# Differential attention of the last two layers moved beside the projection of the banded queries

## The reference

```
h    = rmsnorm(x, g_attn);  proj = h @ w_in          # 2304 columns
qa, ka, va, qb, kb, vb = split(proj)                 # 512, 128, 128, 512, 512, 512
qa, ka, qb, kb = rope(rmsnorm per head of 64)
ya = banded attention(qa, ka, va, sink)              # 8 heads, 2 key heads, blocks |i-j| <= 1 of 128 tokens
s1, s2 = softmax(qb1 kb1'), softmax(qb2 kb2')        # 4 heads, each with two score maps over all 512 tokens
yb = (s1 - lam * s2) @ vb;  yb = rmsnorm(yb, subln) * (1 - lambda_init)
x  = x + [ya, yb] @ w_out
x  = x + (silu(conv(h2 @ w_gate)) * (h2 @ w_up)) @ w_down
```

## Time and profile before

| what | us |
| --- | --- |
| median of 3 runs (2639.18 to 2640.3) | 2639.46 |
| the profiled execution | 2639.93 |
| its span | 2638.1 |
| PE busy | 2494.4 (95%) |
| DVE busy | 1500.0 (57%) |
| ACT busy | 905.5 (34%) |
| POOL busy | 228.1 (9%) |

### The profile page before, as it was taken

One profiled execution on the slowest core, in us unless ns is written; L12 is line 12 of the kernel. 1 busy time (PEld: TensorE's weight loads), 2 busy tenths in 40 slices (PEclk: granted clock), 3 DMA queues, 4 the chain that ended last, 5 costly groups with the idle time before them and its releaser, 6 DMA issues.

```text
span 2638.1 us, 31556 instructions
## 1 busy us (share of the span) xinstructions
PE 2494.4 (95%) x12844; PEld 2050.2 (78%) x12844; DVE 1500.0 (57%) x2120; ACT 905.5 (34%) x1340; POOL 228.1 (9%) x157
## 2 busy tenths in 40 slices
PE   7997999999998799999999779999999888999999
PEld 6766788888876688888887567888888666888887
DVE  5866543434587654343458774646465866554554
ACT  4361322222436133222253553322234354322222
POOL 2002200000210220000042002000002200100000
PEclk9988999999998999999999899999999988999999
DMA  4200122232320012222222001222232200222222
GB/s 172 81 17 1 49 96 100 92 109 87 112 77 33 1 48 96 96 96 96 96 96 96 33 1 64 96 96 96 96 111 97 96 1 1 96 96 96 96 96 96
DMA packets 30241, 205.37 MB, mean 78 GB/s; under 512 B 3344, under 2 KB 3728, under 8 KB 6032
## 3 DMA queue, kind: packets, MB, share of 16 engines
q1 hardware_dynamic: 30096, 203.35, 22.0%
HBM read 201.24 MB, written 2.10 MB: 77 GB/s over the span
## 4 chain that ended last, share of the span: by engine, by line
PE 86%; DVE 9%; DVEq 2%; ACT 2%; issue 1%; POOL 0%; ACTq 0%; DMA 0%; SPq 0%
PE bank L1344 24%; PE bank L1345 24%; PE bank L1346 24%; PE bank L1470 2%; PE bank L1494 2%; PE bank L1451 2%; PE bank L1426 1%; DVE a_conv L917 1%; DVE w_lo L661 1%; PE bank L1632 1%; PE bank L1671 1%; DVE b_p L1216 1%; PE bank L1481 1%; PE bank L1768 1%; DVE neg_max L1204 1%
## 5 line engine op out<-in xcount | busy, mean ns | idle before, releaser
L661 DVE TENSOR_TENSOR w_lo<-w_raw,w_hi 128x2048 fp32r<-128x2048 f32 (+1 forms) x190 | 433.8, 2284 | 418.1 <-ACT w_hi L312 417.9
L1344 PE MATMUL bank<-h_ffn_hi,w_hi 128*128 128x512 f32 x1408 | 548.6, 390 | 0.0
L1346 PE MATMUL bank<-h_ffn_hi,w_lo 128*128 128x512 f32 x1408 | 547.8, 389 | 0.0
L1345 PE MATMUL bank<-h_ffn_lo,w_hi 128*128 128x512 f32 x1408 | 547.8, 389 | 0.0
L312 ACT ACTIVATE w_hi<-w_raw 128x2048 fp32r<-128x2048 f32 (+1 forms) x190 | 360.0, 1895 | 539.9 <-PE bank L1346 491.6
L1346 PEld LDWEIGHTS bank<-h_ffn_hi,w_lo 128*128 128x128 f32 x1408 | 264.3, 188 | 55.1
L1345 PEld LDWEIGHTS bank<-h_ffn_lo,w_hi 128*128 128x128 f32 x1408 | 264.3, 188 | 54.7
L1344 PEld LDWEIGHTS bank<-h_ffn_hi,w_hi 128*128 128x128 f32 x1408 | 264.3, 188 | 54.6
L1344 PE MATMUL bank<-act_hi,w_hi 128*128 128x512 f32 x704 | 273.9, 389 | 0.0
L1345 PE MATMUL bank<-act_lo,w_hi 128*128 128x512 f32 x704 | 273.9, 389 | 0.0
L1346 PE MATMUL bank<-act_hi,w_lo 128*128 128x512 f32 x704 | 273.9, 389 | 0.0
(11 more groups left out here) (303 smaller groups left out, 3561.3 us busy)
## 6 DMA issues: line engine op xcount, KB each, us to landing
w_raw<-weights SPq DMA_DIRECT2D x188, 1024.0 KB, 4.7
residual<-x_in SPq DMA_DIRECT2D x8, 256.0 KB, 6.3
x_out<-residual SPq DMA_DIRECT2D x8, 256.0 KB, 2.1
cst<-consts SPq DMA_DIRECT2D x1, 960.0 KB, 10.6
par_b<-params_b SPq DMA_DIRECT2D x1, 627.0 KB, 11.6
par_a<-params_a SPq DMA_DIRECT2D x1, 244.0 KB, 2.6
w_raw<-weights SPq DMA_DIRECT2D x2, 64.0 KB, 2.0
```

Of the source, the lines that this page charges most:

```text
L661: nc.vector.tensor_tensor(w_lo[s][:, cols], w_raw[s][:, cols], w_hi[s][:, cols].bitcast(F32), ALU.subtract).then_inc(w_ready, 1)
L1344: mm(out, ahi, bhi, start=start, stop=False)
L1345: mm(out, ahi, blo, start=False, stop=False)
L1346: return mm(out, alo, bhi, start=False, stop=stop)
```

## The change

Only the third and fourth layer change, with some set-up at the start.

- The order of the weight groups becomes qb (g0, g0+1), kb (g0+2, 3), vb (g0+4, 5), ka and va (g0+6), qa (g0+7, 8).
- DVE does `tables` behind `split_lo(g0+2)`, and two ropes of qb ahead of `split_lo(g0+3)`.
- The turns of qb stand behind the four half groups of vb, those of kb beside the group of ka and va.
- The differential loop comes first. Behind the PE work of each of its steps 0 to 3 stand two blocks of the qa projection (12 matmuls of 512 columns each). ACT empties them in steps 2 and 3 (`evict_queries`), POOL squares them (`query_squares`, formerly ACT), DVE sums the squares in steps 4, 6, 8, 10 (`stat_a`) and ropes them in steps 5, 7, 9, 11 (`rope_a`); the six turns of ka and qa stand behind steps 11 to 13, in banks 2 and 3.
- Scores use banks 5 and 6 alone up to step 4, then these and 0 and 1 in turn; transposes use bank 7 alone, the output bank 4 alone.
- The banded loop follows, and `norm_diff(3)` and `mix_ready` fall into its step 3.
- lam of both layers is computed once at the start, its four vectors by a transfer of their own; the masks are made from the comparison masks, so `cst` is 128 KB smaller.

The core of the diff (set-up, overlays of tiles and renamed tiles left out):

```diff
 # DVE, layers three and four
+                norm_stats(2 * lay)
+                split_lo(g0 + 2)
+                tables(par, B["b_table_b"], [(B_QB, HD ** -0.5), (B_KB, 1.0)], C_ROPE + 2 * TB * HD, 1)
+                tables(par, B["b_table_a"], [(B_QA, HD ** -0.5), (B_KA, 1.0)], C_ROPE + 2 * TB * HD, 1)
                 if l == 0:
                     norm_bc(2 * lay)
                     for k in range(KT):
                         nc.vector.scalar_tensor_tensor(residual[:, k, :], ...)
+                rope_b(0, 0)
+                rope_b(0, 1)
                 split_lo(g0 + 3)
+                rope_b(0, 2)
+                rope_b(0, 3)
                 split_lo(g0 + 4)
+                rope_b(1, 0)
+                rope_b(1, 1)
                 split_lo(g0 + 5)
+                key_lo(0)
+                rope_b(1, 2)
                 split_lo(g0 + 6)
+                key_lo(1)
+                rope_b(1, 3)
+                key_lo(2)
+                key_lo(3)
                 split_lo(g0 + 7)
+                for m in range(4, 8):
+                    key_lo(m)
+                for i in range(19):
+                    if i < 16:
+                        diff_max(i)
+                    if 1 <= i <= 16:
+                        diff_coef(i - 1)
+                    if i >= 6 and i % 4 == 2:
+                        t = (i - 6) // 4
+                        take_diff(t)
+                        if t >= 1:
+                            norm_diff(t - 1)
+                    if i == 0:
+                        split_lo(g0 + 8)
+                    if i == 3:
+                        split_lo(g0 + 9)
+                    if 4 <= i < 11 and i % 2 == 0:
+                        stat_a((i - 4) // 2)
+                    if 5 <= i < 9 + 3 and i % 2 == 1:
+                        rope_a((i - 5) // 2)
+                    if i == 12:
+                        split_lo(g0 + 10)
+                    if 11 <= i < 14:
+                        for n in (2 * (i - 11), 2 * (i - 11) + 1):
+                            tile_lo(8 + n, tb, ..., banks=(2, 3))
 # ACT, in the differential loop
+                    if i == 1:
+                        split_hi(g0 + 9)
+                    if i in (2, 3):
+                        evict_queries(i - 2)
+                    if i == 3:
+                        split_hi(g0 + 10)
+                    if 11 <= i < 14:
+                        for n in (2 * (i - 11), 2 * (i - 11) + 1):
+                            tile_hi(8 + n, tb, ..., banks=(2, 3))
 # POOL
+                def query_squares(t):
+                    pool.wait_ge(qa_raw, 4 * l + t + 1)
...
+                    nc.gpsimd.tensor_tensor(B["b_qsq"][:, 0:512], q, q, ALU.mult)
+                    nc.gpsimd.tensor_tensor(B["b_qsq"][:, 512:640], k, k, ALU.mult).then_inc(qsq_done, 1)
 # PE
+                pe.wait_ge(rope_ready, 8 + 12 * l + 4)
+                for second in range(2):
+                    enter(g0 + 4 + second)
+                    for half in range(2):
+                        pair_half(g0 + 4, second, half)
+                        m = 2 * second + half
+                        turn(m, base, lambda t: B["b_qb"][:, t, m * P:(m + 1) * P])
+                enter(g0 + 6)
+                token_half(g0 + 6, 0)
+                pe.wait_ge(rope_ready, 8 + 12 * l + 8)
+                for m in range(4):
+                    turn(4 + m, base, lambda t: B["b_kb"][:, t, m * P:(m + 1) * P])
+                    if m == 1:
+                        token_half(g0 + 6, 1)
+                for i in range(19):
...                     # scores of i, transposes of i-2, value product of i-3
+                    if i < 4:
+                        if i % 2 == 0:
+                            enter(g0 + 7 + i // 2)
+                        for n in (2 * i, 2 * i + 1):
+                            pair_block(g0 + 7, n // 4, n % 4)
+                    if 11 <= i < 14:
+                        if i == 11:
+                            pe.wait_ge(rope_ready, 8 + 12 * l + 12)
...                     # two turns
+                pe.wait_ge(do_free, 4 * l + 4)
+                pair_attention(lay, True, ...)
                 w_out(lay, g0 + IN_B, base, 14, B["b_ot_hi"], B["b_ot_lo"], B["b_dm"])
+def diff_banks(i):
+    return (5, 6) if i < 5 or i % 2 == 0 else (0, 1)
```

More of the change, by code:

```diff
@@ L466, in _ @@
             split_hi(1)
+            act.wait_ge(lam_in, 1)
+            nc.scalar.activation(lam[:, 4:8], lam[:, 0:4], ACT.Exp).then_inc(lam_out, 1)
             for lay in range(LAYERS):
@@ new lines, in evict_queries, with key_hi @@
+                def evict_queries(half):
+                    g = g0 + 7
+                    act.wait_ge(bank_done, done_with(g + 1, half))
+                    for t in (2 * half, 2 * half + 1):
+                        j = pair_bank(g, t)
+                        nc.scalar.activation(B["b_qa"][:, t, :], bank[j][:, :], ACT.Copy, scale=rstd[:, t:t + 1]).then_inc(bank_free[j], 1)
+                        act.drain().then_inc(qa_raw, 1)
+                def key_hi(m):
+                    tile_hi(m, tb, (B["b_qt_hi"] if m < 4 else B["b_kt_hi"])[:, m % 4, :])
@@ L599, in _ @@
-                tb = 20 + 18 * l
-                for m in range(6):
-                    tile_hi(m, tb, B["b_kt_hi"][:, m, :])
-                for m in range(8):
-                    tile_hi(6 + m, tb, h_mix_hi[:, m, :])
+                for half in range(2):
+                    evict_pair(g0 + 2, half, lambda t: B["b_kb"][:, t, :], squares=B["b_squares_k"])
+                split_hi(g0 + 5)
+                key_hi(0)
+                split_hi(g0 + 6)
+                key_hi(1)
+                evict_pair(g0 + 4, 0, lambda t: B["b_vb"][:, t, :])
@@ L1193, in _ @@
                         pair_copy(lay, i - 2, window((i - 2) // 4)[1] * P, pts)
-                    if i >= 6 and i % 4 == 2:
+                    if i == 3:
+                        norm_diff(3)
+                        dve.drain().then_inc(mix_ready, 1)
+                    if i >= 6 and i % 4 == 2 and i < 19:
                         normalise(lay, (i - 6) // 4, B["b_r"], B["b_on"])
@@ L1251, in _ @@
-                norm_diff(3)
-                dve.drain().then_inc(mix_ready, 1)
                 for m in range(4):
@@ L1840, in _layer @@
     every = slice(None)
-    parts, at = [], 0
-    for width in plan:
+    parts = []
+    for at, width in plan:
         cs = slice(at, at + width)
```

441 lines of the change are left out of this document (234 added, 207 removed).

## The result

The kernel after takes 2664.09 us (median of 5 runs, 2663.27 to 2676.71) against 2640.3 us (2639.18 to 2640.89) for the kernel before on the same chip: a ratio of 1.010, 95% interval 1.0077 to 1.0122. The change makes the kernel 23.8 us slower; forecast were 22.8.

A forecast was written before the change was run, and what follows sets the result against it. PE was taken as bound outside the differential loop, DVE from its step 4 on. Layer three +15.2 and layer four +7.6 made +22.8 us on 2639.93: 2662 by the median, own range 2652 to 2670, 8 in 10 2644 to 2676.

The forecast's parts named there:

- 2 to the first differential scores: From g0+3 to the first differential scores: PE-bound matmuls and turns, with 2.5 us for low clock; 52.4 us.
- 6 banded loop and tail: Banded loop unchanged at 44.0 us, its tail now exposed at 2.4, norm_diff(3) and take_diff(3) 0.7; 47.1 us.
- 7 w_out's first part: w_out's 12 matmuls and four turns, 6.3 us; the 2.0 us wait for norm_diff(3) gone.
- step 1: Opening, g0+2 to g0+3: ropes ahead of the split make PE wait; 23.8 us in layer three, 14.2 in four.
- Steps 3 and 4: Differential loop: steps 0 to 3 PE-bound, 28.0 us; steps 4 to 16 paced by DVE, added work paid, 70.9 us.
- Rival A: Differential loop: DVE's slack, 10.6 us a layer, takes the added work; 2636 us, faster or level; chance 0.12.
- One sign: From step 4 of the differential loop: mean step over 5 us, DVE busy over 90%, PE under 60%.
- The squares: GpSimd's squares of qa delay DVE in the differential loop: three meetings of 1.03 us, 3.1 us a layer.
- Step 5: Last difference to banded scores: transposes, copy, product and DVE's emptying of the output bank; 3.4 us.
- Rival B: PE falls to the lower clock in the DVE-bound differential steps; +35 us, 2675; chance 0.18.
- Step 8: Start: lam's work, some 3.5 us, hides under PE's first two groups; cost 0, up to 2 us.
- The upper bound: All unknown costs at their high end (clock 4, squares 5, start 2): given as +29.6 us, 2669.

The follow-up runs named there:

- e1_open: The kernel after, with DVE's splits of g0+3 to g0+5 put ahead of part of the ropes in the opening of layers three and four: 2652.31 us.
- e2_norope: The kernel after without the rotation and scaling of the banded queries and keys, one small copy in its place: 2636.5 us, ratio 0.9985 to before.
- e5_pairs: The kernel after with the qa projection's blocks reordered, so that two statistics and rotations a layer fall under PE's projection: 2650.9 us, ratio 1.0041 to before.
- e3_sq2: The kernel after with GpSimd's 128x512 square of qa done twice, same result: 2672.22 us, ratio 1.0121 to before.
- e9_before_sums: The kernel before, with the sums of squares of the first three tokens' differential outputs moved from DVE to ScalarE: 2620.11 us, ratio 0.9915 to before.
- e8_before_norope: The kernel before without the rotation and scaling of the banded queries and keys (two key copies and the statistics stay): 2639.99 us, ratio 0.9993.
- e10_before_splits: The kernel before, with DVE's splits of g0+9 and g0+10 moved from among kb's rotations into the banded loop: 2638.38 us, ratio 0.9986.

## Why the prediction was right

The time came out 2 us from the forecast of 2662, and by the steps that it named (layer three, measured between the rows above):

| step | predicted | measured |
| --- | --- | --- |
| 1 g0+2 to g0+3 | 23.8 | 23.7 |
| 2 to the first differential scores | 52.4 | 51.9 |
| 3 steps 0 to 3 | 28.0 | 29.0 |
| 4 steps 4 to 16 | 70.9 | 69.9 |
| 5 to the banded scores | 3.4 | 5.9 |
| 6 banded loop and tail | 47.1 | 47.4 |
| 7 w_out's first part | 6.3 | 6.1 |
| sum | 231.9 | 233.8 |

Layer four: step 1 14.2 and 14.1, sum 222.3 and 223.7. Between these marks the traces give +17.0 and +9.0, 26.0 us, against 22.8 predicted and 23.8 between the medians. The rest is a matter of the last mark, which the prediction took from the earlier trace rows. At 1590.88 PE of before is at the lower clock (granted 0.50 up to 1595.00), and in after at 1621.20 at the full one: before pays 2.0 us behind the mark in layer three and 0.5 in layer four. At the split of g0+11, before and then after, the surplus of layer three is 15.0 us:

```profile
1371.80 2.29 DVE L661 TENSOR_TENSOR w_lo<-w_raw,w_hi 128x2048 fp32r<-128x2048 f32 x1 [4.06 <-ACT w_hi L312]
...
1603.43 2.29 DVE L661 TENSOR_TENSOR w_lo<-w_raw,w_hi 128x2048 fp32r<-128x2048 f32 x1 [1.32 <-ACT w_hi L312]
```

```profile
1385.09 2.29 DVE L706 TENSOR_TENSOR w_lo<-w_raw,w_hi 128x2048 fp32r<-128x2048 f32 x1 [4.11 <-ACT w_hi L316]
...
1631.73 2.29 DVE L706 TENSOR_TENSOR w_lo<-w_raw,w_hi 128x2048 fp32r<-128x2048 f32 x1 [1.32 <-ACT w_hi L316]
```

So the mechanism is as forecast, but that the number is within 2 us is partly luck: steps that were 3.2 us too short in the two layers and a low clock behind the mark, not reckoned, cancel.

- Step 1: shown. The wait was 11.54 us where 12 were forecast, 2.87 where 3; e1_open takes the layer-four wait and 8.6 us of the other out and gains 11.8 us.
- Steps 3 and 4: shown by e2_norope and e5_pairs. Leaving out four rotations a layer gains 13.8 us a layer, and moving two of them with their sums under PE's projection gains 6.6. Rival A falls with them. One sign was missed by little: DVE was to be busy over 90% from step 4 on and was so 89% of the time; the mean step took 5.4 us and PE was busy 59%, as named.
- The squares: three meetings a layer, as taken. Each costs 0.66 + 0.20 = 0.86 us by the L795 row (1353 against 691 and 484 against 284 ns) where 1.03 was taken. The large and the small product of a rotation are both caught. This trace agrees with the blocking of which the Trainium skill speaks ("SBUF — State Buffer", "SBUF: two separate sides": VectorE with two SBUF operands waits while GpSimd's instruction holds the ports they share); e3_sq2 shows that the price grows with the number of squares, by 0.83 us a meeting.
- Step 5 was short by 2.5 us, the largest miss: 3.4 was taken from a stretch of before at full clock, and the granted clock was 0.67 here. That the clock explains all of it is not shown. Rival B's mechanism is thus at work in a small way: the clock was 0.81 over steps 4 to 16, but PE's slow steps mostly end before DVE's.
- Step 8: layer one's first turn starts at 131.77, in before at 131.21. The difference can't be told from nothing: e5_pairs, with the new start, has that turn at 131.19, and e9_before_sums, with the old one, at 131.37. The cover named there was counted wrong: a pair of groups is 96 matmuls of 512 and 21.7 us, not 192 and 43. It was still enough.
- The upper bound was added up wrong. Clock 4, squares 5 and start 2 give 22.8 + 3.0 + 3.8 + 2 = +31.6, 2671, where +29.6 and 2669 stand; the 2 us of the start are missing. The result does not hang on it.

One thing the prediction left open: why the last rope of kb was late ("until the last rope of kb is done on DVE"). Ahead of e8_before_norope I took it for DVE's load over the whole projection. That run shows that 13 us of this load are free, and e10_before_splits that 4.9 of the 8.75 us were two splits that stood among the last ropes. The contrast is sharper than I had put it: the price of the rotations of qa went from nothing to 27.6 us, more than the whole loss. With the 11.8 us of the opening that makes 39.4, so the change's gains were some 15.6 us (an estimate: it holds if the two prices add, which no run tests), and they were eaten up.

## What to carry to other kernels

Before work is moved, read the idle share of the engine that will do it at both places, and take a wait's releaser apart: leave the suspected work out and see if the wait moves. Filling PE's gap is worth what the loop's other bound allows. Here the fill ran in the four steps that PE then bounded, and what depended on it ran in the thirteen that DVE bounded. And look first at what an idle engine could take from the bounding one: twelve small squares a layer on ScalarE gave 20.8 us in the old order, nearly as much as the whole change lost.

## What the runs showed of the hardware

- A square of 128x512 on GpSimd (1.3 us) beside a DVE product with two operands in SBUF stretched that product from 0.69 to 1.35 us. A product of 128x128 behind it took 0.48 us in place of 0.28, and 1.12 with a second large square.
- ScalarE squares a block of 128x128 and sums it in 0.29 us from one to the next (the sum is read out in a row of its own of 0.20 us, most of it beside the square). Four blocks take 1.3 us, less than DVE's square and sum of the same 512 columns (1.54 us).
- Taking 4.6 us from DVE gave 8.0 and 8.7 us of time where it cut three waits of PE of over 2 us by 1.8 us each: 5.4 and 5.7 us were PE's idle time, and 2.6 and 3.1 us PE's own work, at a granted clock of 0.97 in place of 0.91 and 0.93 in place of 0.88.
